# Attention groups of two by two heads on halves of the array, three groups ahead, with the row maximum fused into the mask

## The chip, the cores and the metric

The kernel runs on one core of one Trainium2 chip. A time is the device time of one execution in microseconds (us). Runs of the kernel before took 953.36, 948.70 and 947.77 us, median 948.7 us. The profile is of a separate execution that took 953.48 us.

The engines of the core are TensorE (PE; its weight loads are shown as PEld), VectorE (DVE), ScalarE (ACT), GpSimd (POOL) and SyncE (SP, which only issues transfers here). They run on their own queues and meet at semaphores.

## What the reference computes

One layer for a prompt of 512 tokens and 8 sample tokens: a wide input projection; three branches (attention over a sliding window of 128, pooling, attention to 256 memory tokens); a gated merge; LayerNorm; a mixture of 16 experts; a second LayerNorm. The change is in the prompt's part of the first and the third branch:

```python
def _gqa_sink_attend(q, k, v, mask, sinks):          # 16 query heads, 4 key/value heads of 64
    s = jnp.einsum('...qkgd,...skd->...kgqs', q, k) * (HEAD_DIM ** -0.5)
    s = jnp.where(mask, s, -jnp.inf)
    m = jnp.maximum(jnp.max(s, axis=-1, keepdims=True), sink)
    p = jnp.exp(s - m)
    p = p / (jnp.sum(p, axis=-1, keepdims=True) + jnp.exp(sink - m))
    return jnp.einsum('...kgqs,...skd->...qkgd', p, v)

def _cross_attend(cq, mk, mv):                       # 4 heads of 64, 256 memory tokens
    s = jnp.einsum('blhd,bmhd->bhlm', cq, mk) * (MEM_HEAD_DIM ** -0.5)
    return jnp.einsum('bhlm,bmhd->blhd', jax.nn.softmax(s, axis=-1), mv)
```

A block of 128 queries sees its own 128 keys and the 128 before them; block 0 sees only its own.

## The kernel before

Each engine has a program written out by hand; nothing plans or reorders it. The stages are: projections (to 142 us), rotation of q and k, the memory's keys and values (to 163 us), the **attention groups** (158 to 313 us), the merge in eight steps, w_out with LayerNorm, routing, experts, and the last LayerNorm.

An attention group is one block of 128 queries by four heads. There are 20 (`groups`): 16 of the window (`swa`: for each pair of key heads, each block b, each of the two key heads h) and 4 of the memory (`mem`, one a block). The four groups with b = 0 are *narrow*: 128 keys; the others are *wide*: 256. For group g the steps are

1. PE, `scores(g)`, L1072: four fp32 matmuls, one a head, q as weights and k streamed, into banks 0 and 1 of PSUM. Two heads of 64 share the 128 rows of z, so the other head's rows are made zero in k (`z[64:]` for even heads, `kodd` for odd, `mkt` and `mkodd` in the memory) and all 128 rows take part.
2. DVE, `scaled(g)`: L1519 scales and adds the mask for four heads at once (L1522 in the memory); `row_max(g)`: L1531 takes the maximum, L1534 negates it and takes in the sink, L1537 prepares the sink's term.
3. ACT, `exps(g)`, L596: one exponential a head, with its sum. DVE, `inverse(g)`: L1547, L1550. POOL, L2123: multiplies by the inverse.
4. PE, L1197: transposes, 128x128 each, into banks 4 and 5. ACT (L684) and DVE (L1660) copy one bank each into `pt`; in a narrow group DVE alone (L1658).
5. PE, L1213: one fp32 matmul of 512 columns for each block of keys, with the v of *two* key heads as its 128 weights columns, into bank 6; half of the 128 rows that come out are used. In the memory (L1218) there is one of 128 columns for each head and key block.
6. ACT takes the used half of bank 6 to fp32r (L688; L606 in the memory), DVE subtracts that from bank 6 for the low part (L1559, L1569, `rest(g)`).

A program counts an fp32 matmul once; the profile has two records for it, each with a weight load. The transposes have one.

In PE's queue the order in group g is: transposes(g), scores(g+2), the product with v(g), `sample(g)`. The last is a share of the 8 sample tokens' attention, small matmuls and transposes (L1089, L1103, L1107, L1123, L1146, L1170). scores(g+2) has one buffer: it waits for the DVE to have read scores(g+1). The product waits for both copies of `pt`, and for the DVE to have done rest(g-1), since bank 6 is one buffer too. `probs` and `stat` have two buffers.

In the last two groups, where no scores are left, PE does the first two of the six products of the first merge step (L1047 to L1049) in their place: product 0 needs the first half of a weight piece, split by DVE in two parts of L1634 (`half_split(0, ...)`, at the ends of DVE's groups 16 and 17); product 1 needs the end of the sample's memory part (`sm_dve`). Product 2 comes behind group 19, and after its third of eight steps it needs the second half (`half_split(1, ...)`: ACT L668 twice at the end of its group 18, DVE L1634 twice behind rest(19)).

Of the kernel before, what the change touches and what calls it, by code (L numbers as in the profile page):

```python
# [13 lines left out]
P = 128  # L14
# [42 lines left out]
def decoder_step(nc, a, o):  # L57

    ctx = ExitStack()
    with ctx:  # L60
# [47 lines left out]
        kodd = at("kodd", OC + 4160, [P, 2, T])  # L108
        mkt = at("mkt", VV + 9216, [P, 2, NMEM])
        mkodd = at("mkodd", ML + 12288, [P, 2, NMEM])  # L110
        probs = [at(f"probs{s}", ML + s * 4096, [P, GRP, 2 * P]) for s in range(2)]
        pt = at("pt", ML + 8192, [P, 2, GRP * P])
        stat = at("stat", TAIL + 512, [P, 2, 8, 4])
        nsink = at("nsink", TAIL + 768, [P, 17])
# [9 lines left out]
        kt = at("kt", ML + 14336, [P, 512])  # L124
# [112 lines left out]
        v_ps, pads, kodd_ok = sem("v_ps"), sem("pads"), sem("kodd_ok")  # L237
# [42 lines left out]
        MEM_ORDER = (0, 2, 1, 3)  # L280
# [223 lines left out]
        def _(ac):  # L504
# [85 lines left out]
            def exps(g):  # L590

                kind, b, h = groups[g]
                s, w = g % 2, P if kind == "swa" and b == 0 else 2 * P
                ac.wait_ge(sc_neg, g + 1)
                for j in range(GRP):
                    last = ac.activation(probs[s][:, j, 0:w], probs[s][:, j, 0:w], ACT.Exp, bias=stat[:, s, 1, j:j + 1],  # L596
                                         accum_out=stat[:, s, 3, j:j + 1])
                if kind == "swa":
# [10 lines left out]
            def sample(i):  # L609
# [17 lines left out]
                if i == 1:  # L627
                    ac.wait_ge(mkt_ps, 1)
                    ac.wait_ge(pads, 5)
                    for r, dst in ((0, mkt), (64, mkodd)):  # L630
                        ac.activation(dst[r:r + 64, :, :], ps[r:r + 64, 3, :].rearrange("p (t m) -> p t m", t=2),
                                      ACT.Copy).then_inc(mkt_out, 1)
# [39 lines left out]
            exps(0)  # L672
            ac.wait_ge(piece_used, N_M + 2)
            for m in range(2):
                ac.activation(mkv[:, m, :], ps[:, (5, 4)[m], :], ACT.Copy).then_inc(mkv_out, 1)
            for g, (kind, b, h) in enumerate(groups):
                if g + 1 < NGR:
                    exps(g + 1)
                if g:
                    sample(g - 1)  # L680
                if not narrow(g):
                    ac.wait_ge(pt_ps, g + 1)
                    ac.wait_ge(o_ps, g)
                    ac.activation(pt[:, 0, :], ps[:, 4, :], ACT.Copy).then_inc(pt_act, 1)  # L684
                ac.wait_ge(o_ps, g + 1)
                if kind == "swa":
                    r, p = 64 * (h % 2), h // 2
                    ac.activation(oahi[r:r + 64, 4 * p:4 * p + 4, b * P:b * P + P],  # L688
                                  ps[r:r + 64, 6, :].rearrange("p (j q) -> p j q", j=4), ACT.Copy).then_inc(o_hi, 1)
                else:  # L690
                    quadrants(ochi[:, :, b * P:b * P + P],
                              ps[:, 6, :].rearrange("p (a t q) -> p a t q", a=2, t=2)).then_inc(o_hi, 1)
# [171 lines left out]
        def _(pe):  # L864
# [190 lines left out]
            def scores(g):  # L1055
# [5 lines left out]
                if g == NKV * NB:  # L1061
                    pe.wait_ge(mkt_out, 2)
                for j in range(GRP):
                    if kind == "swa":
                        p = h // 2
                        k0, w = (0, P) if b == 0 else ((b - 1) * P, 2 * P)
                        q = z[:, ZQ + 4 * p + j, b * P:b * P + P]
                        k = (kodd[:, p, k0:k0 + w] if h % 2 else z[:, ZK + p, k0:k0 + w])
                    else:
                        m, w = MEM_ORDER[j], NMEM  # L1070
                        q, k = z[:, ZC + m // 2, b * P:b * P + P], (mkodd if m % 2 else mkt)[:, m // 2, :]
# [1248 lines left out]
```

## Time and profile before

| | us |
|---|---|
| median of the three runs | 948.7 |
| the profiled execution | 953.48 |
| its span | 951.6 |
| PE busy in it | 851.1 (89%) |
| DVE busy | 544.0 (57%) |
| ACT busy | 437.9 (46%) |
| POOL busy | 162.7 (17%) |
| PE's share of the chain that ended last | 82% |

The span is what the trace covers, from the first to the last record. Durations of PE records overlap, since matmuls are pipelined and their ends are modelled: from one record's start to the next one's start is what a record costs. The profile gives TensorE's granted clock as a share of 2.4 GHz; 0.5 is 1.2 GHz.

### The profile page before, as it was taken

Reading aid. Unit: us, or ns where it says so; the run is one execution under the profiler, and the core shown is the slowest. Engines: PE = TensorE matmul, PEld = TensorE weight load, DVE = VectorE, ACT = ScalarE, POOL = GpSimd, SP = SyncE. Lnnn points to the kernel's source line nnn. Section 1 sums busy time; section 2 is a strip of 40 time slices with the busy share of each in tenths; the row PEclk is TensorE's granted clock in tenths of the full one; section 3 lists DMA queues with packets and bytes.
Section 4 is the critical chain, followed back from the end, with each engine's and each line's share of the span. In section 5 each row is a group of like instructions: output and inputs, shape, how many; then the busy total and the mean of one; then the engine's idle time right before and its main releaser. Section 6 shows DMA issues by size and latency. Waiting matters only on the chain.

```text
span 951.6 us, 13707 instructions
## 1 busy us (share of the span) xinstructions
PE 851.1 (89%) x5330; PEld 753.7 (79%) x5330; DVE 544.0 (57%) x627; ACT 437.9 (46%) x553; POOL 162.7 (17%) x137
## 2 busy tenths in 40 slices
PE   4999988889889899999999998489999999999930
PEld 4999986667669899999999776477888888888820
DVE  3122146766653423333332434759999999999917
ACT  3222222655653323323322213357787788778712
POOL 0095024222221000000000044101111111111012
PEclk9999999999989999999999999589999999999975
DMA  7422212810101221222212453799999999999744
GB/s 284 139 89 88 88 54 75 288 45 1 45 1 54 105 105 67 90 105 105 94 55 76 143 173 101 263 386 406 397 402 391 389 403 392 389 403 389 295 92 132
DMA packets 35563, 180.79 MB, mean 190 GB/s; under 512 B 3591, under 2 KB 11431, under 8 KB 19166
## 3 DMA queue, kind: packets, MB, share of 16 engines
q1 hardware_dynamic: 30278, 161.39, 44.1%
q0 software_dynamic: 5248, 18.91, 7.5%
q8 instruction: 23, 0.38, 0.2%
q14 instruction: 14, 0.11, 0.0%
HBM read 166.78 MB, written 17.94 MB: 194 GB/s over the span
## 4 chain that ended last, share of the span: by engine, by line
PE 82%; DVE 8%; ACT 4%; DMA 3%; issue 2%; POOL 0%; SPq 0%; POOLq 0%; ACTq 0%; DVEq 0%
PE ps L1047 8%; PE ps L1048 8%; PE ps L1049 8%; PE ps L1365 6%; PE ps L1367 6%; PE ps L1366 6%; PE ps L886 4%; PE ps L887 4%; PE ps L888 4%; PE ps L1392 3%; PE ps L1393 3%; PE ps L1394 3%; PE ps L1213 3%; ACT probs L596 2%; PE ps L1353 2%
## 5 line engine op out<-in xcount | busy, mean ns | idle before, releaser
L1819 DVE TENSOR_TENSOR elo<-eraw,ehi 128x2048 fp32r<-128x2048 f32 x96 | 218.1, 2291 | 28.5 <-ACT ehi L763 26.6
L763 ACT ACTIVATE ehi<-eraw 128x2048 fp32r<-128x2048 f32 x96 | 183.0, 1916 | 30.3 <-PE ps L1367 18.3
L1460 DVE TENSOR_TENSOR wlo<-raw,whi 128x2432 fp32r<-128x2432 f32 (+1 forms) x25 | 63.4, 2535 | 153.8 <-ACT whi L515 153.8
L1047 PE MATMUL ps<-xhi,whi 128*128 128x260 f32 x384 | 109.5, 285 | 3.5 <-DVE wlo L1634 3.5
L1048 PE MATMUL ps<-xhi,wlo 128*128 128x260 f32 x384 | 109.2, 284 | 0.0
L1049 PE MATMUL ps<-xlo,whi 128*128 128x260 f32 x384 | 109.0, 284 | 0.0
L1365 PE MATMUL ps<-ehi,xethi 128*128 128x512 f32 x256 | 103.3, 404 | 6.3 <-issue 5.0
L1367 PE MATMUL ps<-elo,xethi 128*128 128x512 f32 x256 | 101.3, 396 | 0.0
L1366 PE MATMUL ps<-ehi,xetlo 128*128 128x512 f32 x256 | 101.1, 395 | 0.0
L515 ACT ACTIVATE whi<-raw 128x2432 fp32r<-128x2432 f32 (+1 forms) x25 | 52.3, 2094 | 90.1 <-PE ps L1049 90.1
L1047 PEld LDWEIGHTS ps<-xhi,whi 128*128 128x128 f32 x384 | 73.0, 190 | 3.7 <-DVE wlo L1634 3.7
L886 PE MATMUL ps<-xhi,whi 128*128 128x260 f32 x256 | 73.1, 286 | 2.0 <-DVE wlo L1460 2.0
L887 PE MATMUL ps<-xhi,wlo 128*128 128x260 f32 x256 | 73.1, 286 | 0.0
L1048 PEld LDWEIGHTS ps<-xhi,wlo 128*128 128x128 f32 x384 | 73.1, 190 | 0.0
L1049 PEld LDWEIGHTS ps<-xlo,whi 128*128 128x128 f32 x384 | 73.1, 190 | 0.0
L888 PE MATMUL ps<-xlo,whi 128*128 128x260 f32 x256 | 72.8, 285 | 0.0
L1365 PEld LDWEIGHTS ps<-ehi,xethi 128*128 128x128 f32 x256 | 48.9, 191 | 19.1 <-issue 6.0
L1367 PEld LDWEIGHTS ps<-elo,xethi 128*128 128x128 f32 x256 | 48.8, 191 | 10.5
L1366 PEld LDWEIGHTS ps<-ehi,xetlo 128*128 128x128 f32 x256 | 49.0, 191 | 9.5
L2170 POOL DMA_INDIRECT f_dram<-yout,dest x16 | 31.7, 1981 | 142.7 <-ACT yout L783 142.7
L2136 POOL TENSOR_TENSOR hall<-hall,lng 104x1024 f32<-104x1024 f32 x4 | 9.6, 2396 | 269.4 <-ACT hall L754 269.4
L1392 PE MATMUL ps<-ehi,hthi 128*128 128x512 f32 x128 | 52.1, 407 | 1.9 <-DVE htlo L1970 1.9
(342 smaller groups left out, 1868.8 us busy)
## 6 DMA issues: line engine op xcount, KB each, us to landing
eraw<-w_gate_in SPq DMA_DIRECT2D x32, 1024.0 KB, 21.6
eraw<-w_up_in SPq DMA_DIRECT2D x32, 1024.0 KB, 22.4
eraw<-w_down_in SPq DMA_DIRECT2D x32, 1024.0 KB, 23.8
raw<-wm_in SPq DMA_DIRECT2D x16, 1216.0 KB, 5.3
raw<-wz_in SPq DMA_DIRECT2D x8, 1024.0 KB, 6.0
raw<-wo_in SPq DMA_DIRECT2D x4, 1024.0 KB, 5.1
h_dram<-hall POOLq DMA_DIRECT2D x5, 416.0 KB, 3.6
f_dram<-h_dram SPq DMA_DIRECT2D x1, 2080.0 KB, 21.3
```

The lines of the kernel that those rows point to most:

```text
L763: ac.activation(ehi[s % 3][:, :], eraw[s][:, :], ACT.Copy).then_inc(ehi_ok, 1)
L886: pe.matmul(out, sh, mh[n], start=start and k == 0, stop=False)
L887: pe.matmul(out, sl, mh[n], start=False, stop=False)
L888: last = pe.matmul(out, sh, ml[n], start=False, stop=stop and k == len(parts) - 1)
L1047: pe.matmul(out, cols(whi[s], q), mh, start=k == 0, stop=False)
L1048: pe.matmul(out, cols(wlo[s], q), mh, start=False, stop=False)
L1049: last = pe.matmul(out, cols(whi[s], q), ml, start=False, stop=k == nk - 1)
L1365: pe.matmul(ps[:, bank, :], xethi[:, k, :], ehi[s[j]][:, w], start=k == 0, stop=False)
L1366: pe.matmul(ps[:, bank, :], xetlo[:, k, :], ehi[s[j]][:, w], start=False, stop=False)
L1367: last = pe.matmul(ps[:, bank, :], xethi[:, k, :], elo[s[j]][:, w], start=False, stop=k == KD - 1)
L1392: pe.matmul(ps[:, 2 + h, :], hthi[:, f, :], ehi[s[j]][:, w], start=f == 0, stop=False)
L1819: ve.tensor_tensor(elo[s % 3][:, :], eraw[s][:, :], ehi[s % 3][:, :].bitcast(F32), ALU.subtract)\
```

## The change

- **Scores.** `kodd` and `mkodd` are gone, with the copies and the zeroing that made them. Each head's matmul takes only its 64 rows: `z[rows, ...]`, rows 0 to 63 for one head, 64 to 127 for the next, in turn; the first writes bank 0, the second bank 1. A group is now two query heads of each of two key heads.
- **Product with v.** Two matmuls for each key block: 64 columns of weights (one key head) with its two query heads' 256 columns of `pt`, into partitions 0 to 63 or 64 to 127 of bank 6. All 128 partitions of 256 columns are used, so steps 6 are 128x256 in place of 64x512.
- **Mask and maximum.** In the window a `tensor_tensor_reduce` for each head does scale, mask and maximum with the sink. In the program it is two instructions, the operation and a read of its 128x1 result. The negation and the sink's term stay.
- **Depth.** `probs` and `stat` have three buffers; scores are issued three groups ahead, ACT's exponentials two groups ahead and in two halves around the copy of `pt`, DVE's inverse two groups ahead at the end of its group. The merge's products 0 and 1 come one group earlier.

```diff
+        probs = [at(f"probs{s}", ML + (0, 4096, 12288)[s], [P, GRP, 2 * P]) for s in range(3)]
-            exps(0)
+            exps(0, range(GRP))
...
+            exps(1, range(GRP))
             for g, (kind, b, h) in enumerate(groups):
-                if g + 1 < NGR:
-                    exps(g + 1)
-                if g:
-                    sample(g - 1)
+                if g + 2 < NGR:
+                    exps(g + 2, range(2))
                 if not narrow(g):
                     ac.wait_ge(pt_ps, g + 1)
                     ac.wait_ge(o_ps, g)
                     ac.activation(pt[:, 0, :], ps[:, 4, :], ACT.Copy).then_inc(pt_act, 1)
+                if g + 2 < NGR:
+                    exps(g + 2, range(2, GRP))
+                if g:
+                    sample(g - 1)
...
+                for j in range(2):
+                    for s in range(2):
+                        rows = slice(64 * s, 64 * s + 64)
+                        if kind == "swa":
+                            k0, w = (0, P) if b == 0 else ((b - 1) * P, 2 * P)
+                            q, k = z[rows, ZQ + 2 * h + j, b * P:b * P + P], z[rows, ZK + h // 2, k0:k0 + w]
...
+                        last = pe.matmul(ps[:, s, 256 * j:256 * j + w], q, k, start=True, stop=True)
...
-                if g + 2 < NGR:
-                    scores(g + 2)
-                else:
-                    merge(0, (g + 2 - NGR,), True)
+                if g + 3 < NGR:
+                    scores(g + 3)
+                elif g + 1 < NGR:
+                    merge(0, (g + 3 - NGR,), True)
...
-                        last = pe.matmul(ps[:, 6, :], v[:, b - nk + 1 + k, (h // 2) * P:(h // 2) * P + P], pt[:, k, :],
-                                         start=k == 0, stop=k == nk - 1)
+                        for s in range(2):
+                            c = (2 * (h // 2) + s) * HD
+                            last = pe.matmul(ps[64 * s:64 * s + 64, 6, 0:2 * P], v[:, b - nk + 1 + k, c:c + HD],
+                                             pt[:, k, 2 * s * P:2 * s * P + 2 * P], start=k == 0, stop=k == nk - 1)
...
-                    ve.scalar_tensor_tensor(probs[s][:, :, 0:w], src[:, :, 0:w], SCALE, mask.broadcast_to([P, GRP, w]),
-                                            ALU.mult, ALU.add).then_inc(sc_row, 1)
+                    for j in range(GRP):
+                        c = 8 * (h // 2) + 4 * (j // 2) + 2 * (h % 2) + j % 2
+                        last = ve.tensor_tensor_reduce(probs[s][:, j, 0:w], src[:, j, 0:w], mask, SCALE, prm[:, c:c + 1],
+                                                       ALU.add, ALU.max, stat[:, s, 0, j:j + 1])
+                    last.then_inc(sc_row, 1)
...
-                if g + 1 < NGR:
-                    inverse(g + 1)
                 if g:
                     sample(g - 1)
                     rest(g - 1)
+                if g + 3 < NGR:
+                    scaled(g + 3)
+                sample_norm(g)
+                if g + 3 < NGR:
+                    row_max(g + 3)
                 if g + 2 < NGR:
-                    scaled(g + 2)
-                sample_norm(g)
-                if g + 2 < NGR:
-                    row_max(g + 2)
+                    inverse(g + 2)
```

On PE, in the wide group 13, the rows stood before as follows (`probs1` is the second buffer of probabilities, `z` holds q and k):

```order
L1197 MATMUL ps<-con_66,probs1_88 128x128 [waits pt_dve,pt_act,sc_nrm]
L1197 MATMUL ps<-con_66,probs1_88 128x128 x7
L1072 MATMUL ps<-kodd_84,z_57 128x256 [waits sc_row]
L1072 MATMUL ps<-kodd_84,z_57 128x256 x3
L1213 MATMUL ps<-pt_89,v_82 128x512 [waits o_hi,o_lo,pt_dve,pt_act]
```

In the changed kernel, group 13 on PE:

```order
L1199 MATMUL ps<-con_66,probs1_86 128x128 [waits pt_dve,pt_act,sc_nrm]
L1199 MATMUL ps<-con_66,probs1_86 128x128 x7
L1075 MATMUL ps<-mkt_84,z_57 128x256 [waits mkt_out,sc_row]
L1075 MATMUL ps<-mkt_84,z_57 128x256 x3
L1217 MATMUL ps<-pt_88,v_82 64x256 [waits o_hi,o_lo,pt_dve,pt_act]
L1217 MATMUL ps<-pt_88,v_82 64x256 x3
```

The scores of the group three ahead (a memory group here) stand where those of two ahead did, and the product is four matmuls of 64 columns of weights.

On PE at the end of the groups, the changed kernel's rows of group 17 (before, L1072's scores stood where product 0 now begins, and product 0 in group 18):

```order
L1199 MATMUL ps<-con_66,probs2_87 128x128 [waits pt_dve,pt_act,sc_nrm]
L1199 MATMUL ps<-con_66,probs2_87 128x128 x7
L1050 MATMUL ps<-xhi_55,whi1_52 128x260 [waits sc_row,lo_split]
...
L1224 MATMUL ps<-pt_88,mkv_83 64x128 [waits o_hi,o_lo,pt_dve,pt_act]
L1224 MATMUL ps<-pt_88,mkv_83 64x128 x7
```

`lo_split` comes from the end of DVE's group 17, behind inverse(19); in PE's queue the product with v of group 17 now stands behind that wait.

On DVE, one wide group of the changed kernel, from one copy of `pt` to the next:

```order
L1664 COPY pt_88<-ps 128x512 [waits o_ps,pt_ps]
L1564 TENSOR_TENSOR oalo_60<-ps,oahi_58 128x2x128 [waits o_hi]
L1525 ISA probs2_87,stat_89<-ps,con_66,prm_67 128x256 [waits sc_ps]
L1525 ISA stat_89 128x1
...
L1538 TENSOR_SCALAR stat_89<-stat_89 128x4 [waits sc_row]
L1540 TENSOR_TENSOR stat_89<-stat_89,prm_67 128x4 [waits sc_neg]
L1552 TENSOR_TENSOR stat_89<-stat_89 128x4 [waits sc_exp]
L1555 RECIPROCAL stat_89<-stat_89 128x4 [waits sc_den]
```

The inverse moved from behind the copy to the group's end, and eight rows of the fused operation stand for L1519 and L1531.

## Rows read from the trace of the kernel before

**Rows 1.** Windows: us, busy us (records) of PE, PEld, DVE, ACT, POOL, clock, DMA, GB/s.
```profile
158.40:313.20 154.80, 133.41 (x804) 107.56 (x804) 95.28 (x186) 79.72 (x253) 36.81 (x23) 0.96 0.21 70
```

**Rows 2.** Waits of PE, 158 to 314 us: total, times, longest.
```profile
PE ps L1213 <- DVE oalo L1559: 12.7, 11, 3.2
PE ps L1047 <- DVE wlo L1634: 3.5, 1, 3.5
PE ps L1197 <- POOL probs L2123: 1.8, 1, 1.8
PE ps L1213 <- ACT pt L684: 1.6, 1, 1.6
PE ps L1218 <- DVE oalo L1559: 1.5, 1, 1.5
```

**Rows 3.** Timeline of PE: start, us, line, tiles, shape, records.
```profile
190.27 1.04 PE L1197 MATMUL ps<-con,probs 128*128 128x128 f32 x8
191.15 1.89 PE L1072 MATMUL ps<-z 128*128 128x256 f32 x8
193.41 1.96 PE L1213 MATMUL ps<-pt,v 128*128 128x512 f32 x4 [0.37 <-DVE oalo L1559]
195.20 0.96 PE L1103 MATMUL ps<-qsp,kt 128*128 128x8 f32 x8
...
223.34 0.65 PE L1139 MATMUL ps<-pnew,v 8*128 8x64 f32 x4
223.92 1.06 PE L1146 MATMUL ps<-pcol,cach_v 128*128 128x8 f32 x8
```

**Rows 4.** Chain that ended last: start, us, engine, tile, line, records.
```profile
185.47 1.74 PE ps L1072 x8
286.60 1.81 PE ps L1218 x16
```

**Rows 5.** Timeline of DVE, one wide group.
```profile
191.35 0.69 DVE L1660 COPY pt<-ps 128x512 f32<-128x512 f32 x1 [1.23 <-PE ps L1197]
192.57 0.69 DVE L1559 TENSOR_TENSOR oalo<-ps,oahi 64x512 fp32r<-64x512 f32 x1
193.29 1.22 DVE L1519 SCALAR_TENSOR_TENSOR probs<-ps,con 128x1024 f32<-128x1024 f32 x1
194.55 1.22 DVE L1531 TENSOR_REDUCE stat<-probs 128x4 f32<-128x1024 f32 x1
196.00 0.16 DVE L1537 TENSOR_TENSOR stat<-stat,prm 128x4 f32<-128x4 f32 x1
```

**Rows 6.** Timeline of ACT, in the same group.
```profile
190.46 0.49 ACT L596 ACTIVATE probs<-probs,stat 128x256 f32<-128x256 f32 x1
190.86 0.19 ACT L596 ACTIVATION_READ_ACCUMULATOR probs<-probs,stat 128x1 f32 x1
190.96 0.49 ACT L596 ACTIVATE probs<-probs,stat 128x256 f32<-128x256 f32 x1
192.65 0.59 ACT L684 ACTIVATE pt<-ps 128x512 f32<-128x512 f32 x1
```

**Rows 7.** Timelines of ACT and DVE at the end of the groups.
```profile
289.23 1.42 DVE L1634 TENSOR_TENSOR wlo<-raw,whi 128x1216 fp32r<-128x1216 f32 x1
301.16 2.33 ACT L668 ACTIVATE whi<-raw 128x1216 fp32r<-128x1216 f32 x2
310.45 2.76 DVE L1634 TENSOR_TENSOR wlo<-raw,whi 128x1216 fp32r<-128x1216 f32 x2
```

**Rows 8.** Windows before and in stretches of low granted clock.
```profile
278.80:282.20 3.40, 3.40 (x34) 3.40 (x33) 1.86 (x3) 2.83 (x10) 0.00 (x0) 1.00 0.00 0
282.20:286.50 4.30, 4.30 (x18) 3.59 (x18) 1.50 (x4) 0.60 (x1) 1.89 (x1) 0.61 0.00 0
309.50:313.20 3.70, 0.30 (x3) 0.09 (x1) 3.59 (x4) 2.42 (x4) 0.00 (x0) 1.00 0.00 0
313.20:317.00 3.80, 3.73 (x19) 3.73 (x20) 0.01 (x1) 0.00 (x0) 0.00 (x0) 0.59 0.63 212
```

More of the change, by code:

```diff
@@ L106, in decoder_step @@
         mkv = at("mkv", VV + 5120, [P, 2, 512])
-        kodd = at("kodd", OC + 4160, [P, 2, T])
         mkt = at("mkt", VV + 9216, [P, 2, NMEM])
-        mkodd = at("mkodd", ML + 12288, [P, 2, NMEM])
-        probs = [at(f"probs{s}", ML + s * 4096, [P, GRP, 2 * P]) for s in range(2)]
+        probs = [at(f"probs{s}", ML + (0, 4096, 12288)[s], [P, GRP, 2 * P]) for s in range(3)]
         pt = at("pt", ML + 8192, [P, 2, GRP * P])
-        stat = at("stat", TAIL + 512, [P, 2, 8, 4])
-        nsink = at("nsink", TAIL + 768, [P, 17])
+        stat = at("stat", TAIL + 512, [P, 3, 8, 4])
+        nsink = at("nsink", TAIL + 928, [P, 17])
         kvrow = at("kvrow", TAIL + 1024, [P, 512])
@@ L278, in decoder_step, with four, sinks @@
         NGR = len(groups)
-        MEM_ORDER = (0, 2, 1, 3)
+        def four(x):
+            return x.rearrange("p (s j) -> p s j", s=2)
+        def sinks(x, h):
+            p, j = h // 2, 2 * (h % 2)
+            return x[:, 8 * p:8 * p + 8].rearrange("p (s j) -> p s j", s=2)[:, :, j:j + 2]
         def narrow(g):
@@ L587, in _, with exps @@
             ac.activation(urow[0:PST + NS, :], ps[0:PST + NS, 7, :], ACT.Copy).then_inc(row_out, 1)
-            def exps(g):
+            def exps(g, heads):
                 kind, b, h = groups[g]
-                s, w = g % 2, P if kind == "swa" and b == 0 else 2 * P
-                ac.wait_ge(sc_neg, g + 1)
-                for j in range(GRP):
+                s, w = g % 3, P if kind == "swa" and b == 0 else 2 * P
+                if heads[0] == 0:
+                    ac.wait_ge(sc_neg, g + 1)
+                for j in heads:
                     last = ac.activation(probs[s][:, j, 0:w], probs[s][:, j, 0:w], ACT.Exp, bias=stat[:, s, 1, j:j + 1],
                                          accum_out=stat[:, s, 3, j:j + 1])
+                if heads[-1] < GRP - 1:
+                    return
                 if kind == "swa":
@@ L628, in sample @@
                     ac.wait_ge(mkt_ps, 1)
[L629 to L632, printed above, removed]
+                    ac.activation(mkt[:, :, :], ps[:, 3, :].rearrange("p (t m) -> p t m", t=2), ACT.Copy).then_inc(mkt_out, 1)
                 if i < NKT:
@@ L684, in _ @@
                     ac.activation(pt[:, 0, :], ps[:, 4, :], ACT.Copy).then_inc(pt_act, 1)
+                if g + 2 < NGR:
+                    exps(g + 2, range(2, GRP))
+                if g:
+                    sample(g - 1)
                 ac.wait_ge(o_ps, g + 1)
[L686 to L689, printed above, removed]
[L690 to L692 removed]
+                out = oahi[:, 2 * h:2 * h + 2] if kind == "swa" else ochi
+                ac.activation(out[:, :, b * P:b * P + P], ps[:, 6, 0:2 * P].rearrange("p (j q) -> p j q", j=2), ACT.Copy)\
+                  .then_inc(o_hi, 1)
                 sample_exps(g - 1)
@@ L1061, in scores @@
                 if g == NKV * NB:
[L1062 to L1071, printed above, removed]
-                    last = pe.matmul(ps[:, j // 2, (j % 2) * 256:(j % 2) * 256 + w], q, k, start=True, stop=True)
+                    pe.wait_ge(mkt_out, 1)
+                for j in range(2):
[4 more added lines that the diff above has]
+                            q, k = z[rows, ZQ + 2 * h + j, b * P:b * P + P], z[rows, ZK + h // 2, k0:k0 + w]
+                        else:
+                            w = NMEM
+                            q, k = z[rows, ZC + j, b * P:b * P + P], mkt[rows, j, :]
+                        last = pe.matmul(ps[:, s, 256 * j:256 * j + w], q, k, start=True, stop=True)
                 last.then_inc(sc_ps, 1)
@@ L1185, in _ @@
             scores(1)
+            scores(2)
             for g, (kind, b, h) in enumerate(groups):
@@ L1652, in _ @@
             row_max(1)
+            scaled(2)
+            row_max(2)
+            inverse(1)
             for g, (kind, b, h) in enumerate(groups):
```

69 lines of the change are left out of this document (24 added, 45 removed).

## The prediction

> **What bounds the kernel now.** I read the windows first: the change touches the stretch from the first scores at 158.4 us to the merge's third product at 313.2, 154.8 us of the span of 951.6 [rows 1]. PE has 133.4 us of work there, DVE 95.3, ACT 79.7, POOL 36.8. So PE is the engine that sets the pace, and it stands for the other 21.4 us. The list of waits says at what: 12.7 us in 11 waits of the product with v for DVE's `rest` of the group before, 1.5 of the same kind in the memory, 1.6 for ACT's copy of `pt`, 1.8 for POOL at the start, 3.5 for the split of the merge's weights at the end [rows 2]. The waits of the middle are 12.7 + 1.5 + 1.6 = 15.8. Everything before and behind the stretch I leave as it is: its instructions and transfers are the same, and what follows begins with products on PE whose inputs have long been there.
>
> The timeline of PE then gives the price of a wide group [rows 3]: transposes 0.88 (190.27 to 191.15), scores 1.74 for 8 records [rows 4], product with v 1.79 for 4 records (193.41 to 195.20), and the sample's part: 8 records of 8 columns in 0.88, at 0.11 each, which is the pace of loading 128 columns of weights, since 8 streamed columns take less. It comes with a load and transposes to about 1.3, and 2.2 where cached values are multiplied. Sum 5.7 to 6.6.
>
> **The change, part by part.**
>
> *Scores.* Before: 16 wide groups at 1.74 [rows 4] and 4 narrow at half, 0.9: 31.4 us. The number of matmuls and their columns stay; time falls only if two on different halves run at once. No row shows two matmuls at once, so the bounds are: no gain (1.0 of the old time) and half. I take something between, for a reason in the order: an fp32 matmul is two records, and both use the same half of the array, so with records 1, 2 on rows 0 to 63 and 3, 4 on rows 64 to 127, only record 3 can run beside record 2, 5 beside 4, and so on. Eight records then take 5 steps in place of 8. Loading stays below that (8 x 0.11 = 0.88 against 1.09). 31.4 x 3/8 = 11.8 us less.
>
> *Product with v.* Before: 12 wide window groups at 1.79 [rows 3], 4 narrow at 0.93, 4 memory groups at 1.81 [rows 4]: 32.4 us. By the same counting: wide 5/8 (8.1 less), narrow 4 records in 3 steps (0.9 less), memory 16 in 9 (3.2 less): 12.2 less. Bounds again none and half.
>
> *Changes of shape.* A group now goes from full array to half rows, to half columns and back, 3 changes, 60 in all. The nearest row is the product of 8 rows by 64 columns, the one place of another shape in the stretch: four records in 0.58 (223.34 to 223.92) [rows 3], against 4 x 0.11 at the loading pace, 0.14 for two changes: 0.07 each. Below it lies nothing; above it, a change that lets a matmul run out first, at most what one small matmul lasts, 0.25 (a row of 8 records lasting 0.96 less 7 x 0.11 [rows 3], rounded up for the last piece). 60 x 0.07 = 4.2 us more. PE's work: 11.8 + 12.2 - 4.2 = 19.8 less.
>
> *DVE.* Removed in a wide group: mask 1.22 and maximum 1.22 [rows 5]. Added: four times operation and read. The fixed part of a DVE row is 1.22 - 2 x (1.22 - 0.69) = 0.16 (a 128x1024 row against a 128x512 one), a column costs 1.04 ns; 256 columns 0.27 + 0.16 = 0.43, less 0.08 since independent rows overlap, and the read one small row, 0.16 with as much overlap [rows 5]: 0.43. Lower bound 0.35 (a read that costs nothing); upper 0.62 (nothing overlaps). ACT's like pair, 0.49 plus a read, has a pitch of 0.50 [rows 6]. I take 0.46. Four are 1.85 for 2.44; `rest` goes from 0.69 to about 0.4 (256 columns a row, not 512). A DVE group: copy 0.61, rest 0.33, fused 1.85, four small rows with their semaphores 0.75: 3.5 us. ACT: exponentials 4 x 0.50 and the sink's 0.1, `pt` and `kt` copies 0.5 each, half of bank 6 0.3: 3.4. POOL 1.89, a whole group ahead now. PE: 0.88 + 1.09 + 1.12 + 1.3 + 0.2 = 4.6, or 5.5. PE still paces, but with 1 us to spare, no longer 2. What each fused row costs is thus covered by PE up to about 0.7 apiece.
>
> *Removed copies and zeroing* (`kodd`, `mkodd`): POOL and DVE stood idle around them, and the first scores were released by the rotation, not by them. Nothing.
>
> *Waits.* The product no longer waits for `rest` in a plain wide group: inverse(g+1), which stood ahead of rest with a wait for ACT, is gone from there, and rest ends 1.0 us behind the transposes, as the scores do. But where DVE has the sample's statistics (groups 5, 6), and ACT its splits and the sample's exponential (12 to 16), the shorter group hides less. I keep 12.3 of the middle's 15.8: 3.5 less. At the start scores(2) now stand ahead of the first transposes and wait for DVE's second group: 1.5 more. At the end three waits are new.
> (a) Product 0 stands behind group 17's transposes. It needs DVE's split at that group's end, which follows inverse(19), which follows ACT's copy and two exponentials: 0.6 + 1.0 + 0.4 + 1.42 [rows 6, 7] = 3.4, with the product with v of group 17 behind it.
> (b) Product 1 needs the sample's memory part, which ACT and DVE do behind their copies: 0.15 + 0.6 + 0.45 + 0.4 = 1.6.
> (c) The product with v of group 19 has no merge product ahead of it, and ACT's copy stands behind its two splits of 2.33 [rows 7]: 0.35 + 2.33 + 0.7 less the transposes' 0.87 = 2.5.
> The last wait of 3.5 shrinks by 0.9, with ACT's and DVE's steps on bank 6 now one row each. Together: -3.5 + 1.5 + 3.4 + 1.6 + 2.5 - 0.9 = 4.6 more.
>
> *Clock.* In the stretch PE ran five times for some 3.5 us at 1.2 GHz, the granted clock of such windows being 0.59 to 0.61 of 2.4, each time behind a stretch in which it idled (309.5 to 313.2: busy 0.30 of 3.70) or did small matmuls of 2 columns (278.8 to 282.2) [rows 8]. Each costs half its length, 1.7. With (a), (c) and thinner work, I expect two more: 3.4 more. Bounds: none more, five more.
>
> Sum: -19.8 + 4.6 + 3.4 = -11.8. The profiled execution took 953.5, 4.8 over the median: it would take 941.7, and the median comes to 948.7 - 11.8 = 936.9.
>
> **The rivals.**
>
> A2. *Both records of a matmul run beside both of the next.* Then both parts halve: 31.9 us less in place of 24.0, 929 by the sum; DVE's and ACT's 3.5 us a group would give some of it back, so 929 to 934. The order of the records speaks against it; nothing in the rows shows how deep the array looks ahead. The Trainium skill ("TensorE: Matmul & The Clock Gate", Measured speedup vs the span model) gives pairs on distinct tiles a start about 4 ns apart, which would bring the kernel here; no run so far has such a pair.
>
> B. *Only one kind of half overlaps, or the changes drain.* For it: each has its own conditions, and rows show neither. Rows only: -11.8 + 4.2 + 4.6 = -3; columns only likewise, and with both but 0.25 a change, 60 x 0.18 = 10.8 more, a third of it lost in waits: -11.8 + 7 = -5. About 945. The Trainium skill ("TensorEngine Tiling (Array Packing)", Key Properties) says that a change of tiling mode drains TensorE. No row shows a change at full stream.
>
> C. *DVE becomes the bound.* If operation and read come to 0.7, DVE's group is 0.61 + 0.33 + 2.8 + 0.75 = 4.5, as PE's, and each hiccup counts: half the middle's waits more, +6: 943; at 0.9 nothing is left of the gain. Against it: no DVE row's fixed part is above 0.2.
>
> D. *The halves take turns.* Then the work grows by 4.2, the middle's waits fall by 7, since PE is slow enough for all, the end's 7.5 come and 0.9 goes: +4 to +5, 953.
>
> E. *They take turns and each change drains* (slower side). 60 x 0.25 = 15 in place of 4.2, three quarters of it on the path: 4.5 + 8 = +12.5, 961. It decides from about 0.17 a change. For it: PE's group would be 7 us, above the old one, and PE is what the others wait for. Against: the one row with another shape shows 0.07.
>
> **How the numbers follow.** My forecast has 0.60, A2 0.09, with its own range 930 to 943: a little more or less overlap, fused rows at 0.35 or 0.62, zero to five slow stretches. B 0.10, C 0.07, D 0.08, E 0.06. The range of 929 to 955 takes in A2 to D, and leaves E and the edges out. One per cent is 9.5 us, about what runs of this kernel can tell from no change: faster means below 939.2. Seven tenths of the forecast's cases lie there, and A2, and a little of C: 0.42 + 0.09 + 0.01 = 0.52. Slower is E and an edge of D: 0.08. The rest is 0.40.
>
> **What would show it.** Eight score records of a wide group in 1.1 us, not 1.74 (D, E) nor 0.9 (full overlap), and product records likewise; the gap at a change of shape 0.07 or 0.25; the fused pair's pitch 0.46; PE's waits for DVE's `rest` below 9 us; a wait of 3.4 us of L1050 for the split in group 17 and one of 2.5 for ACT's copy in group 19; seven stretches at 1.2 GHz; the distance from the first scores to the end of the last split near 143. I would be wrong first of all by the overlap, 24 us in the sum that no row shows, and next by waits in the middle, where four queues with little slack meet.

## The result, and the profile after

| | before | after |
|---|---|---|
| median of 20 runs each, us | 949.07 | 944.66 |
| lowest and highest | 947.77, 953.36 | 939.13, 950.77 |
| ratio | | 0.994 [0.992, 0.996] |
| profiled execution | 953.48 | 944.21 |
| attention stretch in it | 154.8 | 151.0 |
| granted clock in the stretch | 0.96 | 0.81 |

4.4 us less, where 11.8 were forecast: within 1% of before, and inside the range. The profiled execution after lies by its median; that of before lies 4.4 above its own. Of the 9.3 us between the two profiled executions, 3.8 lie in the attention stretch and 2.8 ahead of it, where before spent 6.8 us at 1.2 GHz and after none. Three runs stand in no median below, as slower executions of their kernels: one of before (1737 us), one of e12 (1265) and one of e14 (953.25).

First the windows of the profile after: the stretch that answers to [rows 1], and the six stretches of low clock inside it. Columns are length, busy us (records) of PE, PEld, DVE, ACT, POOL, then clock, DMA share and GB/s.

```profile
155.56:306.60 151.04, 128.04 (x860) 102.42 (x860) 77.71 (x278) 73.70 (x248) 37.96 (x21) 0.81 0.21 72
164.00:171.00 7.00, 5.81 (x26) 3.62 (x26) 5.33 (x26) 4.47 (x20) 1.77 (x2) 0.52 1.06 350
195.00:209.00 14.00, 13.04 (x63) 10.62 (x62) 4.68 (x21) 5.85 (x27) 2.93 (x2) 0.51 0.00 1
219.00:229.00 10.00, 10.00 (x46) 7.65 (x42) 3.84 (x16) 3.17 (x12) 1.89 (x1) 0.50 0.00 0
243.00:250.00 7.00, 7.00 (x34) 5.01 (x32) 2.95 (x11) 3.14 (x12) 1.90 (x1) 0.53 0.00 1
267.00:277.00 10.00, 6.82 (x32) 6.42 (x32) 2.51 (x4) 1.57 (x5) 3.70 (x2) 0.50 0.30 107
284.00:294.00 10.00, 8.58 (x40) 8.21 (x40) 1.46 (x4) 0.84 (x3) 0.00 (x0) 0.50 0.01 2
```

The clock is 0.81 where it was 0.96. Since it has two levels, 2 x (1 - 0.81) x 151 = 57 us of the stretch ran at 1.2 GHz; before it was 12 by the same sum. I call this the **half-clock time**. PE's busy time went down by only 5.4 us, since half of what ran at 1.2 GHz was added to it. In the third and the fourth low stretch PE is busy all the time: the clock was low there though nobody waited.

Before, the low stretches inside the groups were four, each in one of these windows:

```profile
207.00:212.00 5.00, 3.58 (x8) 1.80 (x8) 2.91 (x7) 0.09 (x1) 0.34 (x1) 0.66 0.00 0
224.00:229.00 5.00, 5.00 (x24) 4.50 (x25) 1.76 (x6) 2.65 (x10) 1.35 (x1) 0.66 0.00 0
268.50:273.50 5.00, 4.71 (x15) 2.45 (x16) 2.98 (x6) 1.56 (x2) 1.55 (x1) 0.66 0.00 0
282.00:287.00 5.00, 5.00 (x24) 4.29 (x24) 1.86 (x5) 0.60 (x1) 1.89 (x1) 0.66 0.00 0
```

By the same sum each is 3.4 us (2 x 0.34 x 5.00), 13.6 in all. The six of after are 6.7, 13.7, 10.0, 6.6, 10.0 and 10.0 long. So two more came, and each was two to four times as long.

Now PE's timeline at full clock, in wide groups (it answers to [rows 3]), and one line from a low stretch.

```profile
180.44 1.14 PE L1075 MATMUL ps<-z 64*128 64x256 f32 x8
181.71 1.08 PE L1217 MATMUL ps<-pt,v 128*64 128x256 f32 x8
182.75 1.06 PE L1106 MATMUL ps<-qsp,kt 128*128 128x8 f32 x8
...
184.13 1.04 PE L1199 MATMUL ps<-con,probs 128*128 128x128 f32 x8
185.10 1.13 PE L1075 MATMUL ps<-z 64*128 64x256 f32 x8
...
201.08 1.98 PE L1217 MATMUL ps<-pt,v 128*64 128x256 f32 x8 [0.96 <-DVE oalo L1564]
```

Scores take 1.14 us with the pipeline's tail (1.89 before, [rows 3]), the product 1.04 from its start to the next (1.79). At half clock the same product takes 1.91 to the next start (201.08 to 202.99), more than before the change.

PE's waits in the stretch: total, times, longest. They answer to [rows 2].

```profile
PE ps L1217 <- DVE oalo L1564: 6.9, 4, 2.8
PE ps L1050 <- DVE wlo L1635: 5.5, 2, 3.2
PE ps L1075 <- DVE stat L1525: 3.1, 2, 1.9
PE ps L1224 <- ACT pt L687: 2.9, 2, 2.2
PE ps L1050 <- DVE oclo L1570: 1.4, 1, 1.4
PE ps L1217 <- ACT pt L687: 1.4, 1, 1.4
```

These are 21.2 us, as many as the 21.1 of [rows 2], in other places. The fused pair on DVE, and the end of the groups on PE and ACT, by their timelines:

```profile
163.92 0.48 DVE L1525 CUSTOM_DVE_ANT_0 probs<-ps,con,prm 128x256 f32<-128x256 f32 x1 [0.84 <-PE ps L1075]
164.33 0.08 DVE L1525 DVE_READ_ACCUMULATOR2_ANT stat<- 128x1 f32 x1
164.33 0.48 DVE L1525 CUSTOM_DVE_ANT_0 probs<-ps,con,prm 128x256 f32<-128x256 f32 x1
```

```profile
272.91 0.59 PE L1050 MATMUL ps<-xhi,whi 128*128 128x260 f32 x1 [3.19 <-DVE wlo L1635]
...
302.00 1.09 PE L1224 MATMUL ps<-pt,mkv 128*64 128x128 f32 x16 [2.16 <-ACT pt L687]
```

```profile
299.15 2.31 ACT L672 ACTIVATE whi<-raw 128x1216 fp32r<-128x1216 f32 x2
301.36 0.59 ACT L687 ACTIVATE pt<-ps 128x512 f32<-128x512 f32 x1
```

These are waits (a) and (c) at their foreseen places. So the question is the clock.

Three theories were put to the test. **T1**: matmuls on a half of the array keep the clock down by themselves. **T2**: the halves do not matter as such; what puts the clock down is how little is streamed beside small matmuls and pauses, and the halves shorten the streaming. **T3**: the slow stretches are a matter of phase, so that any shift in time gives another pattern.

### The profile page after: what moved, and what is told of

Its sections match the earlier page's. It is cut to its first block, busy times and chain, and to the rows that moved or that the text cites. A ratio compares the mean times of both kernels' runs of the same rounds, so it can differ in the third digit from the quotient of the medians.

```text
span 942.4 us, 13897 instructions
## 1 busy us (share of the span) xinstructions
PE 841.5 (89%) x5386; PEld 743.9 (79%) x5386; DVE 526.6 (56%) x718; ACT 431.9 (46%) x548; POOL 163.4 (17%) x133
## 4 chain that ended last, share of the span: by engine, by line
PE 84%; DVE 7%; ACT 3%; DMA 3%; issue 2%; SPq 0%; POOL 0%; DVEq 0%; POOLq 0%; ACTq 0%
PE ps L1050 8%; PE ps L1051 8%; PE ps L1052 8%; PE ps L1370 6%; PE ps L1372 6%; PE ps L1371 6%; PE ps L889 4%; PE ps L890 4%; PE ps L891 4%; PE ps L1397 3%; PE ps L1399 3%; PE ps L1398 3%; PE ps L1199 2%; PE ps L1358 2%; PE ps L1250 2%
```

## The experiments

Each run of a kernel lists its mean clock, so its half-clock time over the whole span is 2 x (1 - clock) x span, from all runs whose clock is on record and not only the profiled one. **Plain time** is the run's time less half of that, what would be left if the clock never fell (a bookkeeping figure: a low clock under a wait costs nothing). Medians, us:

| kernel | runs | time | ratio to before | half-clock | plain |
|---|---|---|---|---|---|
| before | 70 | 949.9 | | 91 | 904.0 |
| after | 20 | 944.7 | 0.994 [0.992, 0.996] | 127 | 881.7 |
| e2 scores full | 5 | 942.5 | 0.992 [0.989, 0.995] | 107 | 889.2 |
| e3 product full | 7 | 948.9 | 0.997 [0.995, 0.999] | 110 | 894.3 |
| e4 both full | 10 | 947.4 | 0.997 [0.995, 1.000] | 93 | 901.4 |
| e5 small matmuls twice | 4 | 962.6 | 1.012 [1.007, 1.016] | 146 | 889.6 |
| e6 streaming, fp32 | 9 | 957.6 | 1.007 [1.005, 1.010] | 130 | 892.7 |
| e12 streaming, fp32r | 9 | 954.2 | 1.003 [1.000, 1.006] | 120 | 894.2 |
| e7 late merge | 4 | 939.4 | 0.988 [0.984, 0.992] | 124 | 877.6 |
| e8 filler | 10 | 942.5 | 0.993 [0.991, 0.995] | 111 | 885.8 |
| e14 small filler | 9 | 946.3 | 0.995 [0.992, 0.999] | 127 | 883.2 |
| e9 late, filler | 4 | 936.4 | 0.986 [0.984, 0.988] | 109 | 881.8 |
| e15 late, two fillers | 4 | 937.6 | 0.988 [0.986, 0.991] | 104 | 885.6 |
| e10 late, fillers in memory too | 6 | 941.3 | 0.989 [0.986, 0.993] | 118 | 882.2 |
| e11 only fused, on before | 10 | 949.7 | 0.999 [0.997, 1.001] | 93 | 903.2 |

In the 20 runs of after alone the clock went from 0.940 (939.1 us) to 0.926 (950.8): 28 us more at half clock and 11.6 us more time, 0.42 for each.

**The halves on their own (e1).**

(In the two kernels of this kind several calls are written on one line here.)

```diff
+                def rows(n, halves):
+                    for i in range(n):
+                        for s in halves:
+                            r = slice(64 * s, 64 * s + 64)
+                            mm(ps[:, 4 + s, 0:256], z[r, ZK + i % 4, 0:P], z[r, ZK, 0:256])
...
+                full(60); rows(70, (0, 1)); full(30); rows(70, (0,)); full(30); cols(70, (0, 1)); ...
```

> The changed kernel with a block of extra TensorE work in its last attention group, behind the waits for the copies of pt, whose results nothing reads. Parts, each behind some 13 us of full-array matmuls (fp32, 128x256): 70 pairs on rows 0-63 / 64-127 in turn; 70 on rows 0-63 alone; 70 pairs on columns 0-63 / 64-127; 70 on columns 0-63 alone; 280 transposes of 128x128; 140 matmuls of 8 columns; 8 groups like the changed kernel's (8 transposes, 4 matmuls on halves of rows, 4 on halves of columns, 4 small) and 8 with full-array matmuls in place of the halves. T1 (matmuls on a half of the array keep the clock down): the two single-half parts, and perhaps the pairs, fall to 1.2 GHz for most of their length, while 8-column matmuls do not more than in the kernel before; the group-like part with halves has at least 20 us at 1.2 GHz and the one with full-array matmuls under 7. T2 (halves do not matter, only idle time and short streams do): all parts on halves stay at 2.4 GHz, the 8-column part falls, and both group-like parts alike. T3 (the slow stretches are a matter of phase between engines): nothing falls, since PE never waits here. For the overlap: 140 pairs' records at 0.12 us each if both halves run at once, 0.22 where they take turns; one half alone 0.22 in either case.

Its windows, inside the parts in their order: rows in pairs, one row half, columns in pairs, one column half, transposes, 8 columns, groups with halves, groups with the full array.

```profile
340.00:360.00 20.00, 20.00 (x188) 17.94 (x188) 0.00 (x0) 0.00 (x0) 0.00 (x0) 1.00 0.01 2
385.00:405.00 20.00, 20.00 (x95) 17.32 (x94) 0.00 (x0) 0.00 (x0) 0.00 (x0) 1.00 0.00 1
430.00:440.00 10.00, 10.00 (x96) 6.64 (x94) 0.00 (x0) 0.00 (x0) 0.00 (x0) 1.00 0.00 0
490.00:495.00 5.00, 5.00 (x25) 3.15 (x23) 0.00 (x0) 0.00 (x0) 0.00 (x0) 1.00 0.00 0
515.00:535.00 20.00, 20.00 (x185) 20.00 (x184) 0.00 (x0) 0.00 (x0) 0.00 (x0) 1.00 0.00 1
560.00:600.00 40.00, 40.00 (x190) 40.00 (x189) 0.00 (x0) 0.00 (x0) 0.00 (x0) 0.50 0.00 1
625.00:656.00 31.00, 31.00 (x251) 22.42 (x248) 0.00 (x0) 0.00 (x0) 0.00 (x0) 1.00 0.00 1
670.00:705.00 35.00, 35.00 (x188) 26.86 (x187) 0.00 (x0) 0.00 (x0) 0.00 (x0) 1.00 0.00 1
```

T1 fell: a single half at a time keeps 1.00. What goes to 0.50, with PE busy for 40.00 of 40.00 us, are the matmuls of 8 columns. The Trainium skill ("TensorE: Matmul & The Clock Gate", HAM oscillation — how this bites in real kernels) looks for the cause in idle gaps; this row shows the low clock with none. The two parts with whole groups both stay at 1.00, where T1 had 20 us and more at 1.2 GHz for the one with halves. The rows also settle the overlap. In pairs a record costs 20/188 = 0.106 us on rows and 10/96 = 0.104 on columns, alone 20/95 = 0.211: both records of one matmul run beside both of the other.

The same page of the Trainium skill ("TensorE: Matmul & The Clock Gate", Measured speedup vs the span model) has tiles start some 4 ns apart, and the trace agrees with that full overlap. The parts with whole groups give the price of a change of shape. PE's timeline there:

```profile
625.49 3.14 PE L1080 MATMUL ps<-z 64*128 64x256 f32 x24
628.48 1.07 PE L1100 MATMUL ps<-con,probs 128*128 128x128 f32 x8
629.48 3.14 PE L1080 MATMUL ps<-z 64*128 64x256 f32 x24
```

A group takes 3.99 us (625.49 to 629.48). Its records at the pitches above are 8 x 0.108 of transposes, 8 x 0.106, 8 x 0.104 and 8 small ones at 0.108: 3.41. The rest, 0.58, are three changes: 0.19 each, with whatever the first and the last records of a set lose by having no partner, which no run tells apart. The mix without changes took 5.17 (675.50 to 680.67 on its timeline) against 5.14 of records. The Trainium skill ("TensorEngine Tiling (Array Packing)", Key Properties) has a change of mode drain the engine; the trace agrees that a change costs time: 0.19 is the price here.

**Parts undone (e2, e3, e4).** Scores, then products, then both go back to the full array.

```diff
-                        rows = slice(64 * s, 64 * s + 64)
+                        rows = slice(0, P)
```

```diff
-                        for s in range(2):
-                            c = (2 * (h // 2) + s) * HD
-                            last = pe.matmul(ps[64 * s:64 * s + 64, 6, 0:2 * P], v[:, b - nk + 1 + k, c:c + HD],
+                        last = pe.matmul(ps[:, 6, :], v[:, b - nk + 1 + k, (h // 2) * P:(h // 2) * P + P], pt[:, k, :],
```

> The changed kernel with its score matmuls on all 128 rows (both heads' rows are summed, so the scores are not the reference's); all else as changed. Scores of a wide group go from 0.97 to 1.74 us: 18 groups x 0.77 = 13.5 us more PE work. T1: half-clock time in the attention stretch falls from 58 to about 35 us, 11 us back; with 3 us of PE's waits for DVE's rest gone the time is within 2 us of the changed kernel's 944.7. T2: half-clock time stays near 50; 952. T3: anything between, without order.

> The changed kernel with its product with v on the full array, as before (128 weight columns, 512 columns streamed; half of what comes out is not read, so heads are mixed up); all else as changed. 32.4 - 17.5 = 14.9 us more PE work, at full clock. T1: half-clock time falls from 58 to about 35 us and the time stays within 2 us of 944.7. T2: half-clock time near 50; 953.

> The changed kernel with both score matmuls and product with v on the full array (values not the reference's): what is left of the change is the depth of three, the fused mask and maximum, and the order. 28 us more PE work. T1: half-clock time as before the change, under 20 us (18 us or more given back), PE's waits for DVE's rest nearly gone (6.9 to 1): time 946 to 949. T2: half-clock time stays above 35: 957 or more.

The stretch of e4 by its window, for comparison with after's:

```profile
155.78:307.50 151.72, 132.90 (x804) 110.66 (x804) 77.86 (x278) 73.19 (x248) 37.95 (x21) 0.94 0.21 71
```

The half-clock time falls to 107, 110 and 93 us: with no halves it is that of before (91). The plain time rises by 7.5, 12.6 and 19.7. So the halves do bring some 20 us of plain time, and take 34/2 = 17 back through the clock. With the halves gone from the scores alone the kernel is no slower at all (942.5; the intervals of the two overlap). T1's figures came out here, though e1 had it fall, all but e3's time (948.9, where it named 944.7 give or take 2), and T2's were too high: I had worked them out as if only pauses counted, while under T2 a full-array matmul streams for longer and must hold the clock up too. So these runs give the size, not the cause. PE's waits for `rest`, which were to fall from 6.9 to 1 in e4, were still 5.2. The rest of the change (depth, fusing, order) is e4 against before: -2.5. In e11 the fusing alone, put on the kernel before, gives nothing:

```diff
-            ve.scalar_tensor_tensor(probs[s][:, :, 0:w], src[:, :, 0:w], SCALE, mask.broadcast_to([P, GRP, w]),
+            for j in range(GRP):
+                last = ve.tensor_tensor_reduce(probs[s][:, j, 0:w], src[:, j, 0:w], mask, SCALE,
```

> The kernel before with nothing but the fused scale, mask and maximum (one operation and one read a head, for the two rows over four heads); correct. By the prediction VectorE's group gets 0.8 us shorter under TensorE's pace: nothing or up to 2 us less, half-clock time 91 us as before; pitch of the pair 0.41. If VectorE had been a bound through its late rest: 4 us less or more.

PE's waits for `rest` in the window groups, by the list of waits, went from 12.7 [rows 2] to 10.6, and the time stayed:

```profile
PE ps L1213 <- DVE oalo L1561: 10.6, 10, 3.2
```

**Small matmuls or streaming added (e5, e6, e12).** Behind each of the 12 `sample_scores`, some 0.87 us of PE time (the comments with the names of the runs are added here):

```diff
+                for u in range(4):                                                            # e5
+                    pe.matmul(ps[:, 2, 0:8], kt[:, u * P:u * P + P], kt[:, 0:8], start=True, stop=True)
+                pe.matmul(ps[:, 2, :], kt[:, 0:P], kt[:, :], start=True, stop=True)           # e6
+                for u in range(4):                                                            # e12
+                    pe.matmul(ps[:, 2, :], xhi[:, 0:P], xhi[:, 0:512], start=True, stop=True)
```

> The changed kernel with four more fp32 matmuls of 8 columns (8 records, 0.88 us at 2.4 GHz) behind each of the 12 sample_scores, into bank 2, read by nobody: 10.6 us of work. T1 (halves keep the clock down) has fallen with the part on single halves, which ran at 1.00. T2 (short streams and idle time put the clock down, and the halves only shortened the streaming between them): the half-clock time in the attention stretch rises from 58 to 75 us or more, and the time by 12 or more, to 957 or above. T3 (phase): +8 to +10, the half-clock time as it was, give or take 10.

> The same place and the same TensorE time as in the run before (0.85 us at 2.4 GHz, 12 times, 10.2 us in all), but one fp32 matmul of 128x512, so that the array streams all the time. T2: the half-clock time falls from 58 to 35 us or less, which pays for the added work: time 942 to 948, at least 8 us below the run with short matmuls. T3: as there, 953 to 955, half-clock time near 58.

> As the run with one fp32 matmul of 512 columns behind each of the 12 sample_scores, but four fp32r matmuls of 512 columns (0.86 us in all at 2.4 GHz); correct. That run had a half-clock time of 130 us in the median, 110 in its lowest run, against 146 with short matmuls. T2: 110 or less, time 947 or less. T3 (phase): around 130 again or anywhere between, 955.

Small ones: half-clock time 127 to 146, time 962.6, as T2 has it. Streaming: 130 and 120. The order is T2's (less at half clock than with small ones), the size is not: against the 127 of after, streaming added here took little or nothing off. For e6 T2 named 942 to 948, which only its lowest, profiled run reached (946.5, clock 0.942); the median is 957.6, 5 us below e5 in place of 8. For e12 it named 947 and 954.2 came. T3's 953 to 955 were nearer in both, and the half-clock time of e6 that it named, as it was, came out in the median.

**A filler in every group (e8, e14).**

```diff
                 last.then_inc(o_ps, 1)
+                pe.matmul(ps[:, 4, :], xhi[:, 0:P], xhi[:, 0:512], start=True, stop=True)    # e8, fp32r
+                pe.matmul(ps[:, 4, 0:8], con[:, C_ID:C_ID + P], con[:, C_ID:C_ID + 8], ...)  # e14, fp32
                 sample(g)
```

> The changed kernel with one fp32r matmul of 128x512 (0.22 us at 2.4 GHz, 20 times, 4.4 us in all) ahead of each sample part, into bank 4, read by nobody; correct. T2: half-clock time falls from 58 to about 40 us, time 940 to 943. T3: +2 to +4, half-clock time near 58.

> The kernel with the filler, but with one fp32 matmul of 8 columns (2 records, 0.22 us at 2.4 GHz) in the place of the fp32r matmul of 512 columns: the same shift in time, nothing streamed; correct. T2: half-clock time over the span as in the changed kernel or above (127 to 135 us, where the filler had 111), time 948 to 952. T3 (phase): as with the filler, 111 and 942.5.

The same 0.22 us in the same 20 places: streaming takes the half-clock time from 127 to 111, small matmuls leave it at 127. T2 had named 127 to 135 there and 948 to 952 us; the time was 946.3. The runs of e14 lie from 939.0 to 952.5, the widest spread of all, with half-clock times from 107 to 144, so that its best runs are as good as the filler's. The shift in time alone thus does nothing in the median, and the streaming does. In time the filler's 8 us at half of 16 stand against its own 4.4 of work: 942.5 against 944.7, which the intervals do not tell apart.

**Mixes with no waits at all (e13).**

```diff
+                for n in (6, 8, 10, 14):
+                    for i in range(8):
+                        turn(8); rows(2, (0, 1)); cols(2, (0, 1)); small(n)
+                    full(30)
+                    for i in range(8):
+                        turn(8); full(4); full(2, 512); small(n)
+                    full(30)
```

> The changed kernel with another block of extra TensorE work in its last attention group, read by nobody: mixes of 8 groups each, behind some 13 us of full-array matmuls: 8 transposes, 8 records of scores and 8 of product on halves of the array (some 1.9 us), and then small records of 8 columns (12, 16, 20, 28 of them: 1.3 to 3.1 us); and each time the same with the scores and the product on the full array (3.4 us). No engine is waited for. T2 (the halves shorten what is streamed between small records, and that puts the clock down): as small records grow, the mix with halves falls to 1.2 GHz at a smaller number of them than the mix with the full array; at some number the one is down for most of its length and the other up. If it is only the small records, both fall at the same number. T3 (phase between engines): both stay at 2.4 GHz at every number, since nothing is waited for.

Windows over the last four mixes: 20 small records with halves, 20 with the full array, 28 with halves, 28 with the full array.

```profile
549.40:602.00 52.60, 52.60 (x354) 39.85 (x353) 0.00 (x0) 0.00 (x0) 0.00 (x0) 0.81 0.00 1
616.40:668.00 51.60, 51.60 (x318) 42.22 (x317) 0.00 (x0) 0.00 (x0) 0.00 (x0) 1.00 0.00 1
681.50:745.00 63.50, 63.50 (x410) 50.34 (x409) 0.00 (x0) 0.00 (x0) 0.00 (x0) 0.76 0.00 1
760.50:823.00 62.50, 62.50 (x385) 52.17 (x384) 0.00 (x0) 0.00 (x0) 0.00 (x0) 0.95 0.00 1
```

With the same small records, the mix with halves spent 20 of 52.6 us at 1.2 GHz and the full-array one none; with more of them 30 of 63.5 against 6. With 12 and 16 all stayed at 1.00. The low clock doubles the small records too, and so seven groups with halves took as long (549.39 to 594.79, 45.4 us) as seven of the full array (616.48 to 661.96, 45.5), whose groups are 1.2 us longer at full clock. This is T2 without any other engine: PE was never idle, and no phase between engines could matter.

Two things stay open. The mix with halves was not low throughout: of its eight equal groups some ran at full clock and some did not (their transposes take 1.07 us in some and 1.80 to 1.95 in others), so what a group holds does not settle it alone. And a rival of T2 is untested: that a matmul on half of the array holds the clock up less than one on all of it, beside small matmuls, and not only for a shorter time. Halves with nothing small beside them stay at 1.00 (e1) under either; e2 to e4, e8 and e13 come out the same way by both.

**The merge's products where they were (e7).**

```diff
-                elif g + 1 < NGR:
-                    merge(0, (g + 3 - NGR,), True)
+                elif g + 2 >= NGR:
+                    merge(0, (g + 2 - NGR,), True)
```

> The changed kernel with products 0 and 1 of the first merge step back in groups 18 and 19, as before the change; correct. By the waits: (a) 3.2 us for the split is covered by group 17's product and sample part, (b) 1.4 goes, (c) 2.2 for ACT's copy is hidden by product 1: 5 us or more less, 939 to 940, half-clock time down by one stretch or none. If these waits only stood in for others (the splits of the second half end last anyway): the wait for wlo behind group 19 grows by the same 5 and the time stays at 944 to 945.

PE's waits at the end, now:

```profile
PE ps L1050 <- DVE wlo L1635: 2.3, 1, 2.3
PE ps L1224 <- DVE oclo L1564: 1.2, 1, 1.2
PE ps L1224 <- ACT pt L687: 0.7, 1, 0.7
```

The wait of 3.2 is gone and that of 2.2 too; 5.3 us less time, 4.1 of it plain, from four runs. The other theory, that the last split would take it all, fell: its wait is 2.3, as it was.

**Together (e9, e15, e10).** e9 is e7 and e8 in one; e15 has two fillers a group; e10 adds one ahead of each eight 2-column records of the sample's memory part.

> The late merge products and the filler of one 128x512 fp32r matmul a group together; correct. Over the whole span the changed kernel spends 127 us (median of its runs, twice the missing clock times the span) at 1.2 GHz, the late merge took 4 us of plain time off, the filler added 4 and took 16 of the 127. T2 (the clock falls where too little is streamed, and a little added streaming holds it up): the two gains add up: 881.7 - 4 + 4 + 111/2 = 937. T3 (phase: each shift of the program gives another pattern of slow stretches): half-clock time anywhere from 105 to 130, 934 to 947.

> Late merge products and two fp32r matmuls of 512 columns a group in place of one (4.4 us more work at 2.4 GHz); correct. T2: half-clock time goes on falling, from 109 to about 98, which pays for the work: 935 to 937. T3: no order: 109 give or take 10, 936 to 946.

> As the run before, and one more such matmul ahead of each 8 of the records of two columns in the sample's memory part (16 in all, 3.5 us of work at 2.4 GHz); correct. Those parts ran at 1.2 GHz in every kernel, 32 records in 7.0 us where they need 3.5. T2: half-clock time falls by 10 us more, 935 to 937 in all. T3: +2 to +4 over the run before.

The stretch of e9:

```profile
157.85:296.10 138.25, 121.75 (x880) 98.09 (x880) 77.78 (x278) 73.65 (x248) 37.97 (x21) 0.90 0.23 78
```

138.3 us against 151.0: e9 has the lowest median of the study, 936.4 us, 0.986 of before with an interval wholly below after's; against e7 the intervals overlap. T2 had named 937, and T3's 934 to 947 holds it too. A second filler took the half-clock time from 109 to 104, where T2 had named 98, and the time came to 937.6, which the intervals don't tell from e9. With more in the memory part the half-clock time was 118, against T2. That run was planned on both of the sample's memory parts being at 1.2 GHz; in e9 one took 3.63 us for its 32 records and only the other 6.82.

## Why the prediction was wrong

**The clock** is the term that failed. It had "two more" slow stretches at 1.7 each, +3.4; the half-clock time of the runs rose by 127 - 91 = 36 us, so +18. In the profiled executions the count came true: six stretches inside the groups in place of four, with one more right behind in each, the seven that were named. (I had read five inside; the fifth, at 313.2 [rows 8], is the one behind.) What failed is the length that I gave them: 3.4 us as before, where they were 6.6 to 13.7. The step priced the clock by counting new pauses and took the clock to come back behind each as soon as before. I had a row that said more: PE busy throughout a stretch of 2-column matmuls right before the clock fell [rows 8]. What I missed is that the halves remove streaming, and that the sample's small matmuls beside it stay as long as they were. e4 shows the size (34 us of half-clock time come from the halves); e1 and e13 show that small matmuls beside halves lower the clock with no wait at all. Whether by the shorter streaming alone or also because halves hold the clock up less is not shown. My upper bound, five more stretches or +8.5, did not reach it.

**The overlap** was full, rival A2's case, not 5/8; A2's time of 929 to 934 failed by the clock, as mine did. By e1's pitches it brings the whole 31.9 us. **The change of shape** costs 0.19, not 0.07: 60 are 11.4 in place of 4.2. Together 31.9 - 11.4 = 20.5 less work, against 19.8 forecast: two errors that cancel, by luck. The row of 8x64 matmuls hid the price, since its predecessor had next to nothing in flight.

**DVE.** Four fused pairs at a pitch of 0.41 (163.92 to 164.33), forecast 0.46, below its cover; C did not occur, and e11 confirms that it was worth nothing by itself.

**Waits.** Middle: kept 6.9 + 1.4 + 0.7 (of the 2.9, what is not (c)) = 9.0, forecast 12.3, 3.3 too many. Start: 3.1 for DVE's maximum in place of 1.8 for POOL, +1.3 against +1.5. (a) 3.2 against 3.4, (b) 1.4 against 1.6, (c) 2.2 against 2.5, the last split 2.3 against 2.6. All but the middle were right to a few tenths, and e7 shows that (a) to (c) were on the path and the part of this change that was simply lost.

**The sum by its steps.** Plain time went down by 904.0 - 881.7 = 22.3 where -19.8 + 4.6 = -15.2 was forecast, 7 better; the clock gave 18 back in place of 3.4, 15 worse. -22.3 + 18 = -4.3, where the medians of the times lie 4.4 apart in the first table and 5.2 in the second. The stretch of the profiled executions says the same by other rows [rows 1]: PE's busy time fell by 5.4 where its work fell by 20.5, so the clock put 15.1 on it in place of 3.4; PE stood 23.0 us in place of 21.4, 1.6 more where 4.6 were forecast. The stretch is thus 151.0 us and not 143.

B's 945 is the time that came, by luck: both kinds of half overlap, and a change costs less than its 0.25; the rest was the clock. (Its -3 for one kind alone leaves out the clock's 3.4.) D and E, halves that take turns, did not happen. The forecast's own "I would be wrong first of all by the overlap" named the wrong term.

## What to carry to other kernels

Work taken off TensorE by packing is only worth its time if the clock stays up: look at what small matmuls stand between the packed ones, for they keep their length while the streaming shrinks. Price a lower clock by what remains between them and by how long it will stay low, not by new pauses alone. A cheap streaming matmul in each group lowered the half-clock time (e8: 16 us for 4.4 of work) without a gain in time that the runs can tell, and it did not help wherever it was put (e6, e10, e12). A step that is moved up in a queue takes its wait with it, and all that stands behind it waits too: putting two products back gave 5.3 us, as much as the whole change had (4.4).

## What the runs showed of the hardware

- fp32 matmuls on two halves of the array overlap fully: 0.106 us a record of 256 columns on rows and 0.104 on columns, in pairs, 0.211 alone.
- A change between full array, half rows and half columns at full stream: 0.19 us each, from groups of 3.99 us, the ends of each set included.
- TensorE at 1.2 GHz with no idle time: 8-column fp32 matmuls back to back, 40 us busy of 40, clock 0.50. Matmuls on one half of the array alone: 1.00.
- Half-clock stretches in the attention groups: four of 3.4 us before, six of 6.6 to 13.7 after.
- The mask, scale and maximum operation with its read: 0.405 us apart for 128x256, the read itself 0.08.
- Open: whether a matmul on half of the array holds the clock up less than a full one beside small matmuls; why streaming added behind the sample's scores (e6, e12) did not bring the half-clock time below 120, and why it rose in e10, where the same kind of matmul in each group did lower it. Their runs differ in clock from one to the next, so that the phase in which such a matmul meets the clock's control may play a part; no run here tells.
